# Output stage of a PEER layer: gate tiles loaded for eight experts at a time instead of four

## The reference, cut to what matters

```python
def expert_block(args):
    hx, ix, gx = args
    act = jax.nn.gelu(jnp.einsum('tkd,td->tk', u_tab[ix], hx))
    return jnp.einsum('tk,tkd->td', gx * act, v_tab[ix])
```

## Time and profile before

| | |
|---|---|
| median of 3 runs | 3946.23 us (3944.96 to 3949.29) |
| profiled execution, whole | 3949.65 us |
| its span, first to last instruction | 3948.0 us |
| its granted TensorE clock, mean | 0.969 |
| the output stage in it | 2675.9 us (first gates issued) to 3948.0 us |
| TensorE matmuls busy | 3733.4 us, 95% of the span |
| DVE busy | 2764.4 us, 70% |
| bytes moved by DMA | 846.57 MB |

### The profile page before, as it was taken

One profiled execution on the slowest core, in us unless ns is written; L12 is line 12 of the kernel. 1 busy time (PEld: TensorE's weight loads), 2 busy tenths in 40 slices (PEclk: granted clock), 3 DMA queues, 4 the chain that ended last, 5 costly groups with the idle time before them and its releaser, 6 DMA issues. The chain is left out here.

```text
span 3948.0 us, 54029 instructions
## 1 busy us (share of the span) xinstructions
PE 3733.4 (95%) x18873; PEld 3230.3 (82%) x18873; DVE 2764.4 (70%) x5312; ACT 1270.6 (32%) x1817; POOL 1215.2 (31%) x747
## 2 busy tenths in 40 slices
PE   5999969697999999999999999998999999999998
PEld 2988769355998999989999999996888788888886
DVE  4444256693779999889999996665565666687776
ACT  2311145243222222244444443222232323333333
POOL 0000012111112566555455554661222322223200
PEclk8979989798999999999999999998999999999999
DMA  5225243541112566577777777877888888899976
GB/s 199 68 99 175 94 121 123 192 128 54 33 44 77 200 217 211 195 257 277 285 278 273 277 279 256 292 270 248 277 268 304 269 274 269 285 317 315 315 255 207
DMA packets 396681, 846.57 MB, mean 214 GB/s; under 512 B 34002, under 2 KB 226178, under 8 KB 392850
## 3 DMA queue, kind: packets, MB, share of 16 engines
q1 hardware_dynamic: 309636, 482.80, 37.4%
q0 software_dynamic: 77616, 283.24, 20.8%
q10 hardware_dynamic: 9312, 79.17, 5.0%
HBM read 690.21 MB, written 154.89 MB: 214 GB/s over the span
## 5 line engine op out<-in xcount | busy, mean ns | idle before, releaser
L1715 PE MATMUL ps<-h_hi,u_hi 128*128 128x448 f32 x2048 | 761.4, 372 | 8.6 <-PEq L86 8.6
L1715 PE MATMUL ps<-h_hi,u_lo 128*128 128x448 f32 x2048 | 751.1, 367 | 0.0
L1715 PE MATMUL ps<-h_lo,u_hi 128*128 128x448 f32 x2048 | 750.8, 367 | 0.0
L1949 PE MATMUL ps<-v_hi,a_hi 128*128 128x512 f32 x1768 | 546.9, 390 | 35.3 <-DVE ga_rest L1883 35.3
L1859 POOL DMA_INDIRECT hT<-peer_v,hT x176 | 295.3, 1678 | 821.6 <-DVE hrow L1871 793.1
L1949 PE MATMUL ps<-vw_rest,a_hi 128*128 128x512 f32 x1768 | 545.6, 390 | 0.0
L1949 PE MATMUL ps<-v_hi,ga_rest 128*128 128x512 f32 x1768 | 545.0, 390 | 0.0
L1596 POOL TENSOR_TENSOR u_lo<-uw,u_hi 128x1024 fp32r<-128x1024 f32 x126 | 326.0, 2587 | 583.8 <-ACT u_hi L1517 583.8
L1879 DVE TENSOR_TENSOR ga<-ga,gt 128x512 f32<-128x512 f32 (+1 forms) x256 | 159.4, 623 | 438.3 <-DMA ga<-s_d 435.3
L1829 ACT ACTIVATE v_hi<-vw 128x1024 fp32r<-128x1024 f32 x256 | 271.2, 1059 | 578.9 <-DMA vw<-peer_v 573.7
L1522 ACT ACTIVATE so<-ps 128x448 f32<-128x448 f32 x256 | 139.7, 546 | 953.1 <-PE ps L1715 953.1
(11 more groups left out here) (336 smaller groups left out, 6008.1 us busy)
## 6 DMA issues: line engine op xcount, KB each, us to landing
vw<-peer_v SPq DMA_DIRECT2D x256, 512.0 KB, 5.4
uw<-u_T SPq DMA_DIRECT2D x128, 512.0 KB, 3.8
s_d<-so SPq DMA_DIRECT2D x256, 224.0 KB, 4.6
gates_d<-big ACTq DMA_DIRECT2D x28, 2048.0 KB, 6.8
gt<-gates_d SPq DMA_DIRECT2D x32, 1024.0 KB, 7.6
ga<-s_d SPq DMA_DIRECT2D x128, 256.0 KB, 5.8
gt<-gates_d SPq DMA_DIRECT2D x32, 768.0 KB, 5.4
ga<-s_d SPq DMA_DIRECT2D x128, 192.0 KB, 5.2
```

Source lines behind the costliest of these rows:

```text
L1715: mm = pe.matmul(g.ps[4 + 2 * s + b][:, 0:HALF], u[s][:, k, :], h[:, k, b * HALF:(b + 1) * HALF], start=(k == 0 and i == 0), stop=(k == KD ...
L1949: mm = pe.matmul(g.ps[2 * t + q][:], aa[s][:, rows_], v[s][:, q * 512:(q + 1) * 512], start=(begin and i == 0), stop=(end and i == 2), ski ...
```

## The change

The gates are loaded for `SPAN` = 8 blocks at a time, into two tiles `gt` of twice the width (8 x 32 numbers for each chunk and row, so 32 KB of each partition for both instead of 16 KB). SP issues them at every second group of four blocks, still in the fourth slot ahead of its `vw` and `a`; the loop body is now four groups instead of two, since two gate tiles cover 16 blocks. In DVE the wait and the slice follow the new count. The number of blocks, the products and all other transfers stay.

```diff
+    SPAN = 2 * RING
-        gt = [sb(f"gt{i}", [P, TA * P // CT, RING * CT]) for i in range(2)]
+        gt = [sb(f"gt{i}", [P, TA * P // CT, SPAN * CT]) for i in range(2)]
...
-                sp.dma_start(gt[s][:, 0:(c1 - c0) // CT, :], g.gates_d[c0 // CT:c1 // CT, :, bass.ds(e, RING), :].rearrange("j p b t -> p j (b t)")).then_inc(g_loaded[s], 16)
-
-            def loads(p, e, i, last=False):
+                sp.dma_start(gt[s][:, 0:(c1 - c0) // CT, :], g.gates_d[c0 // CT:c1 // CT, :, bass.ds(e, SPAN), :].rearrange("j p b t -> p j (b t)")).then_inc(g_loaded[s], 16)
+
+            def loads(p, e, m, last=False):
                 c0, c1 = span(p)
                 for s in range(RING):
                     sp.wait_ge(o_done, p * NE + e + (s + 1))
-                    if s == RING - 1 and not last:
-                        gates(p, e + RING, 1 - i)
-                    elif s == RING - 1 and p == 0:
-                        gates(1, 0, 1 - i)
+                    if s == RING - 1 and m % 2 == 0:
+                        if not last:
+                            gates(p, e + SPAN, 1 - m // 2)
+                        elif p == 0:
+                            gates(1, 0, 1 - m // 2)
...
-                with sp.Fori(0, NE // RING // 2 - 1) as j:
-                    loads(p, j * (2 * RING), 0)
-                    loads(p, j * (2 * RING) + RING, 1)
-                loads(p, NE - 2 * RING, 0)
-                loads(p, NE - RING, 1, True)
+                with sp.Fori(0, NE // (4 * RING) - 1) as j:
+                    for m in range(4):
+                        loads(p, j * (4 * RING) + m * RING, m)
+                for m in range(4):
+                    loads(p, NE - (4 - m) * RING, m, m >= 2)
...
-                dve.wait_ge(g_loaded[n // RING % 2], 16 * (n // RING // 2 + 1))
+                dve.wait_ge(g_loaded[n // SPAN % 2], 16 * (n // SPAN // 2 + 1))
...
-                dve.tensor_tensor(by, by, gt[n // RING % 2][:, 0:(c1 - c0) // CT, s * CT:(s + 1) * CT], ALU.mult).then_inc(a_ready, 1)
+                dve.tensor_tensor(by, by, gt[n // SPAN % 2][:, 0:(c1 - c0) // CT, n % SPAN * CT:(n % SPAN + 1) * CT], ALU.mult).then_inc(a_ready, 1)
```

## The result

The changed kernel takes 4025.88 us (median, 4022.54 to 4030.31) against 3947.76 us (3944.96 to 3950.34) for the kernel before: 1.0202 times as long, 95% interval 1.0186 to 1.0218, so 78 us or 2.0% slower. The prediction was 3958 with a range to 3970: the sign was right, the size six times too small.

The account below looks back on a forecast made before the run. TensorE was taken as the bound, the DMA engines close behind. Added waits of 2.4 + 2.4 + 2.5 + 5 = +12.3 us gave 3958.5 us set on the median, range 3945 to 3970.

Parts of the forecast that it names:

- the sign: Whole kernel: the change makes it slower, given 0.60, against 0.35 for the same and 0.05 for faster.
- The limits: Output stage: TensorE waits when W exceeds 13.55 us in pass 0 or 9.75 us in pass 1.
- W: Output stage: time from the issue of the gates to DVE's product L1879, which waits for `a` to land.
- term 3: Other gates loads kept in pass 0: five of 15 exceed the limit by 0.16 to 0.69 us; taken as +2.5 us.
- The price of a piece: Gates loads: a 1024-byte piece costs 46 ns, from the line through 27 (512 bytes) and 83 (2048): 19 ns more.
- so W grows by it: Gates queued before `vw` and `a`: W grows by the longer pieces' cost, 2.4 us in pass 0, 1.8 in pass 1.
- term 4: Pass 1: seven of 15 kept gates loads exceed the limit, +7.3 us; less 1.7 at block 207; taken as +5.
- third rival (double price): Gates loads: a 1024-byte piece costs 54 ns, twice a 512-byte one; +29 us, 3975 us; chance 0.05.
- Row gathers: Rival, both passes: gathers slip into the longer gates burst packet by packet; +17 to +20, 3963 to 3966 us; chance 0.12.
- Start of the stage: Output stage's first gates load, ahead of everything: TensorE's first wait of 18.85 us grows by 2.4 us.
- Block 67: Middle of pass 0, where TensorE already waits 9.97 us behind a gates load: the wait grows by 2.4 us.

Follow-up runs that it names:

- the late slot: Kernel before, with SP waiting one block more in every second group of pass 1 before issuing the fourth slot's gates, `vw` and `a`: 4003.1 us, ratio 1.0154.
- two loads of four in one slot: Changed kernel with each gates load split into two loads of four blocks, issued one right after the other in the same slot: 4005.1 us, ratio 1.0152.
- wide tiles: Kernel before with the two gate tiles twice as wide, only the first half of each row used, loads unchanged: 3946.3 us, ratio 1.0000.
- the run with the gates last: Changed kernel with the gates of eight blocks issued in the same slot but behind its `vw` and `a`: 3991.7 us, ratio 1.0104.

## Why the prediction was wrong

**The limits held.** W over 13.55 us in pass 0 and over 9.75 in pass 1 make TensorE wait. By them W = 13.71 gives 3.96, and 3.97 was seen; the late slot confirmed it by itself. (The sum written there for pass 1 comes to 9.73, and a packet of q10 in the earlier trace rows takes 113 / 725 = 156 ns, not 166; neither moves the result. The lowest W of the five loads of term 3 was 11.23, block 75, and not 11.31.)

**The price of a piece was right and did not settle W.** A packet of 1024 bytes takes 46 to 48 ns once a load is under way, as the line between the neighbours gave. The step that failed is the next one, "so W grows by it" (term 4 of the sum): 1.8 us more in pass 1. In the quiet part it grew by 4.5. Of this 2.7 are the strides: the pieces lie 16384 bytes apart and chunks 2 MB, and with rows 17408 bytes apart the load has neither the slow first microseconds nor the late last pieces. A price for each piece times the number of pieces says nothing of such a tail. The row of the kernel before that I had, 27 ns, was taken from the middle of a load; the start of the stage had shown 91% x 64 us / 1903 = 31 ns for pieces of 512 bytes, and I read it as a queue that is not quite full.

**Beside the gathers W grew by as much, for two reasons.** The mean W in us of the gates loads issued with blocks 131, 139 and so on to 219, where the row gathers run, and with 227, 235 and 243, after them:

| kernel | mean W, 131 to 219 | mean W, 227 to 243 (quiet part) |
|---|---|---|
| before | 8.43 | 7.11 |
| prediction (before + 1.8) | 10.2 | 8.9 |
| changed | 12.98 | 11.55 |
| changed, padded | 11.59 | 8.84 |
| changed, no row gathers | 10.96 | 11.52 |
| changed, padded, no row gathers | 8.91 | 8.88 |
| two loads of four in one slot | 12.31 | 9.75 |

The kernel before had gathers in its W already, 1.3 us of it. The prediction missed 2.8 us; padding takes away half of this, and the other half is what gathers add to the longer burst beyond that. The last row says it again: its pieces cost twice 27 ns, which the prediction's third rival (double price) put at 3975, and its W in the quiet part came out by that price, but it took 4005.

**Row gathers were a right rival at too small a size.** I gave the case with them +17 to +20 in all, a quarter of the 78 measured, by "some bursts meet one more". The run without them is 45 us faster, with padding 30. Taken away alone the two causes give 50 and 45 us, together 80 and not 95: what lies under the limit is worth nothing, so the second finds less to save.

**The clock was left out of the sum.** I priced each wait by its length. Pass 1 to block 224 lost 33 us to waits and 19 to the slower clock after them. No wait of the kernel before in pass 1 was longer than 1.95 us, and none was followed by a slow clock; but behind the wait of 9.97 at block 67 pairs of 1.19 us stood in my own rows.

**Term by term.** Start of the stage: +2.4 predicted, +4.3 measured (23.17 for 18.85), since the gathers now meet the first load (the two queues from 2687 to 2691 us above; in the kernel before that load is through 6 us after its issue, just as the gathers' packets begin). Block 67: +2.4 predicted, -1.0 measured in one execution; the unchanged loads gave 8.91 with wide tiles and 9.49 with the late slot, so this term is nothing. The prediction itself had said that the gates there wait mostly for the other queue's packets, and then their own price need not show; that was not tried. Other waits of pass 0: +2.5 predicted, +3 measured. Pass 1: +5 predicted, 37 and 19 measured. The stage of the two profiled executions differs by 70 us: TensorE waits 46 us more in it and is busy 24 us longer for the same number of matmuls, 19 of these in pass 1 up to block 224. The later start of the stage in this execution (2678.6 for 2675.9 us) is not the change's: it varied between 2670 and 2683 us over the runs.

**What the prediction had right:** the sign; the wait behind `a` in the same queue as the mechanism; no wait of pass 1 in a group without gates beyond what the next slot inherits; nothing in the wider stride of DVE and nothing in the fewer issues on SP.

What stays open: why equal strides slow the reads in the first 3 to 4 us of a load and let its last pieces come so late, and which of the two distances does it, that of the rows or that of the chunks, since the padding changed both. That the row gathers are what made the run with the gates last miss was argued, not tried.

## What to carry to other kernels

Before bunching transfers in a queue, compute for the work that stands behind them the slack in microseconds, and compare it with the whole burst as it will drain beside the other queues and to its last piece, not with its price on a quiet queue; if the slack is a few microseconds, split the load over the slots rather than joining it. Price a wait of the bound engine by its length and by the slow clock that follows it. When pieces are read from a scratch whose rows lie a power of two apart, try padded rows: it is one number in a shape, and it was worth 50 us where bursts were over their limit and nothing where they were not.

## What the runs showed of the hardware

- Reads of 1024-byte pieces 16384 bytes apart moved at 67 ns a packet (218 a microsecond) from 1.5 to 4.5 us after the issue of a load and at 48 later, and the last of the load's 1536 pieces landed 2.8 us after nine tenths of them. 17408 bytes apart they moved at 48 in the same part of the load, and the last piece landed 0.7 us after nine tenths. Pieces of 512 bytes gained 0.3 to 0.5 us of W by the same padding.
- After a wait of 3.97 us TensorE was granted 0.56 of its clock for 3.9 us, then all of it. In the idle time itself the granted clock was still 1.00. After a wait of 1.95 us there was no fall. After one of 2.01 us there was, after one of 2.70 there was none; in the run without row gathers one of 1.94 us was followed by a fall. The length of a wait alone doesn't tell it.
- With twice the bytes in the gates load, the same number of packets, W went from 7.06 to 11.58 us on quiet queues and to as much as 14.7 with row gathers beside it, where the slack was 9.75.
